# Attention stage of a two-layer decoder: where the dense steps stand among the transposes

## The reference

```python
def forgetting_attention(q, k, v, c):      # q, k after rms_norm per head
    ...
    def one_block(args):
        qb, cb, blk = args
        logits = jnp.einsum('bhtd,bshd->bhts', qb, kf) + cb[..., None] - c_t[:, :, None, :]
        q_pos = blk * FOX_BLOCK + jnp.arange(FOX_BLOCK)
        logits = jnp.where(key_pos[None, :] <= q_pos[:, None], logits, -jnp.inf)
        probs = jax.nn.softmax(logits, axis=-1)
        return jnp.einsum('bhts,bshd->bthd', probs, vf)
    o = lax.map(one_block, (q_blocks, c_blocks, jnp.arange(nb)))

def fox_mixer(x, w_in, b_f, q_norm_g, k_norm_g, w_out):
    ...
    o = forgetting_attention(q, k, v, c)
    o = o * jax.nn.silu(z.reshape(B, S, FOX_HEADS, FOX_DH).astype(F32))
    return o.reshape(B, S, FOX_W).astype(x.dtype) @ w_out
```

## Time and profile before

| | |
|---|---|
| median of 3 runs | 1883.04 us (1881.57 to 1883.49) |
| profiled execution: time | 1883.0 us |
| its span, first to last instruction | 1881.0 us |
| mean granted TensorE clock | 0.974 |
| TensorE busy | 1751.0 us, 93% of the span |
| VectorE / ScalarE / GpSimd busy | 927.2 / 754.8 / 238.4 us |
| fox_attention | about 1152 to 1646 us |

### The profile page before, as it was taken

One profiled execution on the slowest core, in us unless ns is written; L12 is line 12 of the kernel. 1 busy time (PEld: TensorE's weight loads), 2 busy tenths in 40 slices (PEclk: granted clock), 3 DMA queues, 4 the chain that ended last, 5 costly groups with the idle time before them and its releaser, 6 DMA issues. The chain is left out here.

```text
span 1881.0 us, 29102 instructions
## 1 busy us (share of the span) xinstructions
PE 1751.0 (93%) x11308; PEld 1318.2 (70%) x11308; DVE 927.2 (49%) x1748; ACT 754.8 (40%) x1239; POOL 238.4 (13%) x199
## 2 busy tenths in 40 slices
PE   7999999999999877979989998999999999899798
PEld 5777777777777656868877887655666555588687
DVE  3767677675766625653340300344444444575523
ACT  3436354363544514132231311555555555440411
POOL 2212122221222100200000000111110110012000
PEclk8999999999999978989999999999999999999899
DMA  5121010310101004132130201111111101050311
GB/s 128 46 55 35 24 46 13 57 34 24 46 13 54 4 1 146 56 96 67 40 114 0 71 22 43 36 36 36 43 29 40 41 19 43 1 168 34 104 51 48
DMA packets 113799, 92.34 MB, mean 49 GB/s; under 512 B 19776, under 2 KB 95744, under 8 KB 113664
## 3 DMA queue, kind: packets, MB, share of 16 engines
q1 hardware_dynamic: 113664, 90.49, 16.8%
HBM read 81.99 MB, written 8.49 MB: 48 GB/s over the span
## 5 line engine op out<-in xcount | busy, mean ns | idle before, releaser
L424 PE MATMUL gdn_unit<-part_hi,gdn_w_hi 128*128 128x512 f32 x512 | 235.7, 460 | 0.0
L426 PE MATMUL gdn_unit<-part_hi,gdn_w_lo 128*128 128x512 f32 x512 | 202.0, 394 | 0.0
L425 PE MATMUL gdn_unit<-part_lo,gdn_w_hi 128*128 128x512 f32 x512 | 200.9, 392 | 0.0
L1952 DVE CUSTOM_DVE_ANT_0 fa_probs<-fa_scores,fa_decay 128x896 f32<-128x896 f32 (+7 forms) x128 | 97.0, 758 | 122.4 <-PE fa_scores L1769 77.8
L1721 PE MATMUL fa_unit<-part_hi,fa_w_hi 128*128 128x512 f32 x256 | 115.5, 451 | 17.2 <-ACT fa_qk L1868 15.8
L789 DVE SCALAR_TENSOR_TENSOR x<-gdn_raw,gdn_taps,x 128x512 f32<-128x512 f32 x144 | 123.6, 859 | 5.1
L1901 ACT ACTIVATE fa_probs_t<-fa_turned 128x512 f32<-128x512 f32 (+1 forms) x96 | 52.3, 545 | 158.9 <-PE fa_turned L1786 158.5
L426 PEld LDWEIGHTS gdn_unit<-part_hi,gdn_w_lo 128*128 128x128 f32 x512 | 96.2, 188 | 21.6
L391 POOL TENSOR_TENSOR gdn_w_lo<-ring,gdn_w_hi 128x1024 fp32r<-128x1024 f32 x31 | 75.1, 2424 | 269.4 <-ACT gdn_w_hi L604 269.4
L1895 ACT ACTIVATE fa_probs<-fa_probs,fa_top 128x896 f32<-128x896 f32 (+7 forms) x128 | 99.4, 777 | 21.8 <-DVE fa_top L1952 18.1
L424 PEld LDWEIGHTS gdn_unit<-part_hi,gdn_w_hi 128*128 128x128 f32 x512 | 97.2, 190 | 14.7 <-issue 3.6
(11 more groups left out here) (290 smaller groups left out, 3560.3 us busy)
## 6 DMA issues: line engine op xcount, KB each, us to landing
ring<-in_gdn_w_in_dram SPq DMA_DIRECT2D x32, 512.0 KB, 4.1
ring<-in_ple_w_gate_dram SPq DMA_DIRECT2D x32, 256.0 KB, 3.0
ring<-in_fox_w_in_dram SPq DMA_DIRECT2D x32, 256.0 KB, 3.2
ring<-in_fox_w_in_dram SPq DMA_DIRECT2D x16, 512.0 KB, 4.8
fa_decay<-c_rows_scratch SPq DMA_DIRECT2D x64, 128.0 KB, 3.0
in_x_tile<-in_x_dram SPq DMA_DIRECT2D x8, 512.0 KB, 6.5
gdn_g_bc<-g_rows_scratch SPq DMA_DIRECT2D x8, 512.0 KB, 8.7
m_old<-in_x_dram SPq DMA_DIRECT2D x8, 512.0 KB, 3.6
```

Of the source, the lines that this page charges most:

```text
L424: pe.matmul(out, w_hi[:, j % 2, k, :], xh[:, k, ts], start=(k == 0), stop=False)
L425: pe.matmul(out, w_hi[:, j % 2, k, :], xl[:, k, ts], start=False, stop=False)
L426: mm = pe.matmul(out, w_lo[:, j % 2, k, :], xh[:, k, ts], start=False, stop=(k == KT - 1))
```

## The change

In TensorE's list of fox_attention the two turns of a side now stand together, and the two dense steps that stood one behind each turn stand together behind them. At e = 7, where only the first turn had a dense step behind it, the one step stands behind both. The number of instructions and all waits stay as they are. The iteration it = 0, which has no turns, keeps its order; the lists of the other engines are the same.

```diff
                     for side in sides(e - 1):
-                        for by in range(2):
-                            if p >= 0:
+                        if p >= 0:
+                            for by in range(2):
                                 turn(p, e - 1, side, by)
-                            if e < NT - 1 or by == 0:
-                                fill(1)
+                        fill(2 if e < NT - 1 else 1)
```

## The result

The changed kernel takes 1888.91 us in the median (1887.09 to 1891.04), the kernel before 1883.19 (1881.57 to 1885.47): 1.0031 times as long, 95% interval 1.0020 to 1.0043. Forecast were 1887.6 us and a range of 1882 to 1893. The sign and the size hold: +5.7 us measured, with an interval of +3.8 to +8.1, and +4.6 forecast. The profiled execution took 1891.0 us, its span 1887.0.

A forecast was written before the change was run, and what follows sets the result against it. TensorE, busy for 93% of the span, was taken as the bound, so the order of its work counts; 4.6 + 0 + 0 = +4.6 us on 1883.0 gave 1887.6 us, range 1882 to 1893.

The forecast's parts named there:

- The cost of the wait: Transposes leave the bank handover at e = 2, 4 and 7, so idle grows: 0.66 us a pass, 4.6 us in seven.
- The switches and the joint: At 88 places in the attention, joining two groups of transposes saves and costs nothing: 0.
- Rival A: Each joint of two transpose groups costs 0.02 to 0.06 us: 1889 to 1893 us; chance 0.20.
- rival B: The switch between transposes and dense steps is really saved, up to 0.08 us a place: 1880.6 us; chance 0.12.
- Waits that come sooner: The second turn's group runs one dense step earlier; its waits for exponents and VectorE's takes were to cost 0.
- the tight place in the last pass: Second side of e = 1, waiting for VectorE's take: 0.2 us to spare; if gone at 4 places, 0.8 us.
- The handover as a fixed length: Bank's last matmul to next step takes 1.23 to 1.24 us start to start, whatever transposes stand in it.
- rival C: The bank handover is not a fixed 1.24 us but shrinks when ScalarE is idle sooner: 0, 1883 us; chance 0.04.
- Nothing comes back: VectorE's earlier takes in the attention give TensorE no time back, the gate's 7.8 us included: 0.
- The clock: The attention stage keeps its granted clock of 1.00 with eight transposes in a row: cost 0.
- rival D: The clock falls to 1.2 GHz behind each joined group, for its dense steps: 100 us, 1988 us; chance 0.02.

The follow-up runs named there:

- turns_inside: Kernel before, with both turns put inside the bank handover at e = 2, 4 and 7, ScalarE's copy ahead of its take; 1881.73 us, 0.9991 of before.
- copy_twice: Kernel before, with ScalarE's copy of the projection bank made twice, the second signalling; 1902.23 us, 1.0097 of before.
- all_but_sites: Changed kernel with the old order kept at the three handover places of a pass, 64 of 88 joints standing; 1883.34 us, 0.9998 of before.
- shifted_pairs: Changed kernel with four dense steps instead of three at e = 0 and none instead of one at e = 7; 1868.05 us, 0.9918 of before.
- shifted_turns: Kernel before, in its old order, with four dense steps instead of three at e = 0 and none at e = 7; 1866.67 us, 0.9911 of before.
- sites_only: Kernel before, with turns joined only at the three handover places of a pass, 24 of 88 joined places; 1889.06 us, 1.0030 of before.
- after_again: The changed kernel repeated unaltered beside the other runs on one chip; 1889.13 us, 1.0033 of before.

## Why the prediction was right

- The cost of the wait: forecast 0.66 us a pass, measured 0.67 in the second pass (58.54 us from score(0) to score(0) before, 1250.50 to 1309.04; 59.21 after, 1252.91 to 1312.12), 4.6 in the seven (409.3 and 413.9), 4.5 in the stage. The handover is 1.22 to 1.25 us start to start with none, one, two and three transposes in it, and in turns_inside with four, five and seven (the last from 1321.80 to 1323.03). The waits are 17.6 us in 21 times, as written down. copy_twice shows that it is ScalarE's copy that ends them.
- The switches and the joint: forecast 0, measured 0.00 to 0.01 us a place (score(1) to score(2), two joints: 6.37 us before, 6.39 after), and all_but_sites shows no difference over 64 joints. Rival A is refuted by it: its least cost, 0.02 us a joint, would be 1.3 us over 64 joints, which the interval of the medians (up to +1.3) leaves just possible, but the stage is longer by 0.0, and by 0.1 us the other way between shifted_pairs and shifted_turns. So is rival B, since nothing is saved. The reading that decided this one was the transposes' 0.03 us in the earlier trace rows: whoever had looked at the dense step alone, 0.77 against 0.69 us, would have forecast a gain. The prediction also says that the weight loads ran ahead in the earlier trace rows, which those rows don't show; the loader's timeline does, with the load of the four at 1346.06 and their matmuls at 1346.29:

```profile
1346.06 0.59 PEld L1786 LDWEIGHTS fa_turned<-ident,fa_probs 128*128 128x128 f32 x4
```

- Waits that come sooner: TensorE's waits for the exponents stay at 0.6 us, those for VectorE at the gate's 7.8; the tight place in the last pass cost nothing that shows.
- The handover as a fixed length: rival C, by which it would shrink when it is empty, is refuted by the same 1.23 to 1.24 us with nothing in it.
- Nothing comes back: right. VectorE waited 76.3 us for the transposes ahead of its takes, 97.6 before, and 98.2 us for score, 77.8 before: it got its work sooner and stood idle later.
- The clock: rival D is refuted, 1.00 in the stretch with eight transposes in a row.
- The total came out 1.1 us above the sum and 1.2 above what the stage grew by. The runs sites_only and after_again have an excess too, 5.5 us for 4.5 and 4.6 in the stage; all_but_sites has none. It is inside each interval, and whether it is scatter stays open.

What I missed is not in the sum, but near it. The prediction took the 13.2 us for what there is to win or lose in the handover, and didn't see that moving the count of dense steps by one, in either order, hides it altogether, nor that the place is worth more than its idle time says.

## What to carry to other kernels

Where one engine fills a single buffer and another must empty it before the next round, look up what stands in that gap, by the number of the step, before reordering anything around it: here 24 of 88 reordered places made the whole cost, and a shift of the count by one step was worth nearly four times what the order cost. Read the gap start to start, with and without work in it; if its length stays the same, that work is free there, and moved out it costs its full time (here 0.11 us for each transpose). The regrouping itself, with equal sums of start-to-start times, was neutral here, however different the single steps looked.

## What the runs showed of the hardware

- A group of 128 x 128 transposes showed no fixed price between dense steps: to the next start it took 0.03 us with one, 0.35 with four and 0.79 with eight, about 0.11 us for each more, and the switch back to dense (0.08 us longer first interval) is returned by the group's own short start.
- The handover of a 128 x 512 PSUM bank from TensorE over a ScalarE copy and back took 1.22 to 1.25 us start to start, of which the copy is 0.60; a second copy made it 1.85 to 1.88 us at 23 of 24 places, and 2.14 at one.
- A stage in which up to eight transposes stood together, with dense pairs of 1.5 us between them, kept the granted clock of 1.00.
